# FFN 2 of a diffusion block: the high-weight ring read 64 bytes further on, and one scratch tile fewer

## What is computed

```
h  = h  + 0.5 * gate * swiglu(modulate(rmsnorm(h)),  ffn_w_in[0], ffn_w_out[0])     # FFN 1, latent
hc = hc + 0.5 * gate * swiglu(modulate(rmsnorm(hc)), ffn_w_in[0], ffn_w_out[0])     # FFN 1, context
p  = modulate(rmsnorm(.)) @ w_in                      # latent and context
y  = concat(pool_mixer(p), gated DeltaNet of 8 heads(p)); h = h + gate * (y @ w_out)
h  = h + 0.5 * gate * swiglu(modulate(rmsnorm(h)), ffn_w_in[1], ffn_w_out[1])       # FFN 2, latent only
out = rmsnorm(h, final_g)

swiglu(u): a, b = split(u @ w_in);  (silu(a) * b) @ w_out        # 2048 -> 2 x 5632 -> 2048
gdn_gate_out: o * rsqrt(mean(o*o) + eps) * o_norm_g * silu(z)    # per head
```

## The kernel before

| tensor | use | start | start modulo 128 |
|---|---|---|---|
| `x` (high and low) | moving, FFN 1 and heads | 16672 | 32 |
| `hth`, `htl` | moving, FFN 1 | 184608, 192800 | 32 |
| `yh`, `yl` | moving, `w_out` | 16736, 33120 | 96 |
| `x2` | moving, FFN 2 up | 49504 | 96 |
| `ha`, `hb`, `hc` | moving, FFN 2 down | 16736, 153952, 180576 | 96 |
| `wh` | high weights, all stages | 115488 | 32 |
| `wl` | low weights, all stages | 131872 | 32 |

## Time and profile before

### The profile page before, as it was taken

The page is one execution under the profiler, slowest core; times in us unless marked ns, Lnnn a source line. Parts: engine busy times, 40 slices in busy tenths (PEclk is TensorE's granted clock), DMA queues, the critical chain, the costliest instruction groups (busy, mean ns, idle before and its releaser), DMA issues. The chain is left out here.

```text
span 2837.3 us, 41545 instructions
## 1 busy us (share of the span) xinstructions
PE 2789.0 (98%) x15367; PEld 2355.4 (83%) x15367; DVE 1636.9 (58%) x2089; ACT 997.7 (35%) x1475; POOL 212.2 (7%) x363
## 2 busy tenths in 40 slices
PE   6999999999999999999999999999999999999998
PEld 4688888888888888888888888878998888888887
DVE  5567777777777752222226766755675555555444
ACT  3222222222222221112214555544454444444443
POOL 0000000000000000000001112554120000000001
PEclk9999999999999999999999999999999999999999
DMA  9867677677988956655663666686556666666664
GB/s 380 304 208 225 204 227 221 202 229 260 325 315 303 324 180 193 193 176 178 197 192 93 174 193 196 198 257 182 157 180 193 189 189 192 190 189 191 192 191 143
DMA packets 410340, 604.67 MB, mean 213 GB/s; under 512 B 52960, under 2 KB 303840, under 8 KB 401520
## 3 DMA queue, kind: packets, MB, share of 16 engines
q1 hardware_dynamic: 361824, 419.52, 48.0%
q10 hardware_dynamic: 48400, 183.63, 19.3%
HBM read 560.02 MB, written 43.02 MB: 213 GB/s over the span
## 5 line engine op out<-in xcount | busy, mean ns | idle before, releaser
L2032 DVE TENSOR_TENSOR wl<-raw,wh 128x1024 fp32r<-128x1024 f32 x638 | 786.6, 1234 | 938.2 <-ACT wh L1535 937.5
L1535 ACT CAST wh<-raw 128x1024 fp32r<-128x1024 f32 x638 | 667.8, 1048 | 1443.3 <-PE ps L791 915.3
L789 PE MATMUL ps<-x,wh 128*128 128x512 f32 (+1 forms) x2312 | 900.9, 390 | 0.1
L791 PE MATMUL ps<-x,wl 128*128 128x512 f32 (+1 forms) x2312 | 896.6, 388 | 0.0
L790 PE MATMUL ps<-x,wh 128*128 128x512 f32 (+1 forms) x2312 | 896.6, 388 | 0.0
L791 PEld LDWEIGHTS ps<-x,wl 128*128 128x128 f32 x2312 | 434.1, 188 | 89.8
L789 PEld LDWEIGHTS ps<-x,wh 128*128 128x128 f32 x2312 | 434.2, 188 | 88.1 <-issue 0.5
L790 PEld LDWEIGHTS ps<-x,wh 128*128 128x128 f32 x2312 | 434.4, 188 | 87.1
L2229 DVE SCALAR_TENSOR_TENSOR acc<-abuf,cT,acc 128x1024 f32<-128x1024 f32 x300 | 371.4, 1279 | 19.1 <-DMA abuf<-in_w_ada 18.8
L797 PE MATMUL ps<-x,wh 128*128 128x512 f32 x1408 | 348.0, 392 | 0.3
L797 PEld LDWEIGHTS ps<-x,wh 128*128 128x128 f32 x1408 | 253.2, 188 | 46.6 <-issue 1.1
(11 more groups left out here) (322 smaller groups left out, 2358.1 us busy)
## 6 DMA issues: line engine op xcount, KB each, us to landing
raw<-in_ffn_w_in SPq DMA_DIRECT2D x704, 256.0 KB, 3.2
raw<-in_ffn_w_out SPq DMA_DIRECT2D x176, 512.0 KB, 3.7
abuf<-in_w_ada ACTq DMA_DIRECT2D x64, 1024.0 KB, 6.9
abuf<-in_w_ada ACTq DMA_DIRECT2D x96, 512.0 KB, 3.9
x<-d_h ACTq DMA_DIRECT2D x80, 512.0 KB, 3.3
ada_t<-in_ada SPq DMA_DIRECT2D x64, 512.0 KB, 9.6
raw<-in_w_in SPq DMA_DIRECT2D x128, 256.0 KB, 3.5
raw<-in_w_out SPq DMA_DIRECT2D x32, 512.0 KB, 5.0
```

The costliest lines, as they stand in the source:

```text
L789: mm(out, ah, bh, start=first, stop=False, skip_group_check=reopened)
L791: return mm(out, al, bh, start=False, stop=last, skip_group_check=reopened)
L1535: nc.scalar.copy(wh[:, t % HL, :], raw[:, t % RAW, :]).then_inc(hi_done, 1)
L2032: tt(tl, raw[:, t % RAW, :], th.bitcast(F32), ALU.subtract).then_inc(lo_done, 1)
```

## The change

Three things are changed.

1. `wh` gets a parent `wh_all`, 448 bytes longer than the ring, behind a new filler `apart5` of 64 bytes. Tiles below `T_FFN2` lie in `wh_all` from byte 448 on, tiles of FFN 2 from byte 0 on (`wh_ffn2`). The new starts are: `wh` 116000 (residue 32 modulo 128 as before), `wh_ffn2` 115552 (residue 96, that of the moving tiles), `wl` 132384 (residue 32 as before, so 64 bytes off the moving tiles of FFN 2). All tensors declared after the ring move by 512 bytes, `hb` and `hc` among them; no residue modulo 512 changes but that of the high weights in FFN 2. Tile 376 is in slot 0, and slot s of the new place overlaps only the old slots s and s-1, which hold tiles that the existing wait on `tile_used` already covers.
2. `osq` is gone. `out_squares(h)` writes the squares into `yt`, after a new wait for `y_lo` of head h-1.
3. The dummy square root that fetches ScalarE's function table writes to `n_rstd[:, 3:4]`.

```diff
-        wh = sb("wh", [P, HL, TILE], F32R)
+        sb("apart5", [P, 16])
+        wh_all = sb("wh_all", [P, 112 + HL * TILE], F32R)
+        wh = wh_all[:, 112:].rearrange("p (h n) -> p h n", h=HL)
+        wh_ffn2 = wh_all[:, 0:HL * TILE].rearrange("p (h n) -> p h n", h=HL)
         wl = sb("wl", [P, HL, TILE], F32R)
...
-                osq = sb("osq", [P, 2, P], stack=two)
...
+        def high_weights(t):
+            return (wh_ffn2 if t >= T_FFN2 else wh)[:, t % HL]
...
                 def high(q, kk):
-                    return mm(ps[:, bank + q, :], wh[:, t % HL, w], operand(kk), start=kk == 0, stop=kk == k_all - 1)
+                    return mm(ps[:, bank + q, :], high_weights(t)[:, w], operand(kk), start=kk == 0, stop=kk == k_all - 1)
...
-                nc.scalar.copy(wh[:, t % HL, :], raw[:, t % RAW, :]).then_inc(hi_done, 1)
+                nc.scalar.copy(high_weights(t), raw[:, t % RAW, :]).then_inc(hi_done, 1)
...
             def out_squares(h):
                 act.wait_ge(HS["o_set"], at("o_set", h, 8))
+                if h:
+                    act.wait_ge(HS["y_lo"], at("y_lo", h - 1, 1))
                 for q in range(2):
-                    i = fn(osq[:, q, :], o[:, q, :], ACT.Square, accum_out=oss[:, q:q + 1])
+                    i = fn(yt[:, q * P:(q + 1) * P], o[:, q, :], ACT.Square, accum_out=oss[:, q:q + 1])
...
-            fn(osq[:, 0, 0:1], ones, ACT.Sqrt)
+            fn(n_rstd[:, 3:4], ones, ACT.Sqrt)
...
-                th, tl = (eh[:, t - T_HEADS], el[:, t - T_HEADS]) if t in SPARE else (wh[:, t % HL], wl[:, t % HL])
+                th, tl = (eh[:, t - T_HEADS], el[:, t - T_HEADS]) if t in SPARE else (high_weights(t), wl[:, t % HL])
```

## The result

The changed kernel takes 2846.64 us (median of 22 runs), the kernel before, run beside it, 2840.21 us (22 runs): a ratio of 1.0022, 95% interval 1.0016 to 1.0028, or 6.4 us more. The forecast was 1.5 us less. The median of before was 2844.55 us in the three runs shown ahead of the prediction and 2840.2 us in 22, so absolute times are compared only with before runs made beside them.

The account below looks back on a forecast made before the run. TensorE's matmul rate in FFN 2 was taken as the bound. `high` saving 0.04 us a round over 33 rounds, say 1.5 us, with `low` and the rest 0, gave 2844.55 - 1.5 = 2843.0 us; range 2832.5 to 2850.5.

Parts of the forecast that it names:

- TensorE's rate in FFN 2: In FFN 2 TensorE is busy without a gap for 728 us, so only the rate of its matmuls moves the end.
- 2.4 ns for each `high`: FFN 2: the same residue for weights and moving data takes settled `high` matmuls from 229.1 to 226.7 ns.
- The rule of the Trainium skill: TensorE's two read ports are independent and it never waits on anyone, so the new address would be worth nothing.
- I take the mixture as unchanged, 0: `low` runs in FFN 2 keep their mix of 113 and 118 ns: 0, between 5.0 us saved and 4.6 lost.
- the transition of `high`: FFN 2: `high` runs behind the four `low` runs at 118 ns each pay 0.027 us before reaching the good rate.
- Rows 7: Profile rows from the heads, all at one residue: leaving a 256-column run costs 0.027 us before 512-column matmuls reach the good rate.
- slower rival: FFN 2: all `low` runs at 118 ns lose 4.6 us, full `high` transitions 1.3: 5.9 us more, 2850.5 us; chance 0.13.

Follow-up runs that it names:

- layout_only: The changed kernel, but FFN 2 keeps using the high ring's own place, so only the rest of the change stays in; ratio 1.0001 to the kernel before.
- high_only: The changed kernel without the `low` matmuls of FFN 2, their part of the sum left out; one run, 2622.78 us.
- counts_of_three: The kernel before, addresses kept, with FFN 2's `high` runs cut to 6, 9 and 9 matmuls, eight `low` between them; ratio 0.9984 to the kernel before.
- both_moved: The changed kernel with the `low` ring also moved to the residue of the moving tiles in FFN 2; ratio 1.0025 to the kernel before.
- rings_32: The kernel before with both weight rings 32 bytes further on in all stages, the tensors behind them kept at their residue; ratio 1.0195 to the kernel before.
- all_32: The kernel before with a 32 byte filler ahead of the first tensor, so all tensors move together; ratio 0.9995 to the kernel before.

## Why the prediction was wrong

**What held.** TensorE's rate in FFN 2 is all that counts, and nothing else of the change costs time (layout_only). The residue does matter, by 2.4 ns for each `high` in step (226.7 ns in high_only, 229 before). The rule of the Trainium skill that was weighed, "SBUF — State Buffer", section "Who interferes with whom", by which the two read ports of TensorE are independent, would have given 1.000 for every experiment on addresses. The measured ratios of 1.0022, and of 1.0195 for 32 bytes, are against that here. Whether the two reads wait on each other, or something else depends on their distance, no run shows.

**The step that failed: "I take the mixture as unchanged, 0"** for `low`. The new `high` runs of eight and sixteen hand over only the worse of the two paces. Measured: 7.53 us a round instead of 7.40, 4.3 us over the stage; the prediction had 4.6 us as its bad end. It was taken as the middle of two ends, without asking at which place of its own rhythm a `high` run stops. The trace of before held the answer: a run that stops after a whole 226, 229, 232 is followed by the 113 pace. With the new address that rhythm of threes is gone, and with it what the good `low` runs had ahead of them. counts_of_three shows the cause from the other side: when each run is made to stop after a whole three, with the same addresses and the same matmuls, all `low` runs are at 113.

**The term that was mis-sized: the transition of `high`.** It was 4 x 0.027 = 0.11 us a round, for the runs behind a `low` run at 118. The measured sum is 14.73 - 14.51 = 0.22 us a round, or 2.3 us over the stage more than before, where the prediction had 1.3 less. Most of that follows from the first step: with all seven `low` runs at 118 all seven `high` runs pay, which makes 0.19. The rest is the price. With both rings at one residue it was 0.027 (both_moved), as in the earlier trace rows. With `low` 64 bytes off it is 0.031 in the mean of seven, and far from equal: 0.06 for the run of sixteen, with ten uneven distances, and 0.04 and 0.01 in turn for those of eight. Rows 7, where both matmuls around the hand-over have the same residue, gave the mean nearly, and not the pattern. That the good rate itself comes with the address was right (high_only).

**A slip in the slower rival.** The prediction let it decide only when more than about six of the seven `low` runs take the 118 pace. By its own terms a fifth one is enough: `low` then takes 0.04 us more a round, and `high`, with five transitions, 14.65, 0.01 less than before.

**The rival that came true** is the slower one, given 0.13: 5.9 us by its working, with all `low` at 118 and the full transition after each run, against 6.9 us by the rounds and 6.4 by the medians. Its place and both its terms are what the traces show. Its mechanism, that the last `high` of a run is out of step because it loads a `low` block, is not: in the run from 2237.3 us of the changed kernel the last distance, from the last `high` to the first `low`, is 226 ns like those ahead of it, and `low` goes at 118 behind it all the same.

**What stays open.** Why the distance of 0, 32 or 64 bytes gives these rhythms, and why `low` at 64 bytes has two paces, was not settled; the runs show which place leads to which pace and no more. Other distances were not tried. That 128 bytes is the right measure is shown in part only. In rings_32 the tensors `hth` and `htl` of FFN 1 lie 128 bytes further from the rings, modulo 512, than `x` does, and the mean is 233.3 ns for both, with another pattern (230, 232, 238 against 231, 235, 232, 235). At 0 and 64 bytes no run tells a rule that repeats every 128 bytes from one that repeats every 512.

## What to carry to other kernels

A rate that is read from a long run of equal matmuls is not the rate of a short run between others: look at how long the transition lasts, in matmuls, and compare it with the run. When a stage repeats in a rhythm with unequal pieces, ask first what the good pieces have ahead of them; here another order of the matmuls, with the same number of them, won 0.16%, while the address that looked better lost 0.22%. And to price an address, keep the layout and switch only that (layout_only), since a filler moves much else.

## What the runs showed of the hardware

At the granted clock of 1.00 (2.4 GHz) the distance between fp32r matmuls of 512 columns depends on how far the weights and the moving data start apart, taken modulo 128 bytes: 226.7 ns at 0, 229 at 64 (a repeated 226, 229, 232), 233 at 32. For 256 columns it is 120 at 0, 113 or 118 at 64, and 117 at 32 (0.93 us for eight). Moving everything together by 32 bytes changes neither the rate at 0 nor the rhythm at 64 (all_32). A pace of TensorE can persist over more than a hundred matmuls (13.19 us for 112), and which of two it is can depend on where in its rhythm the run before stopped.
